# Low weight parts of every fourth chunk by a negated copy on ScalarE and an accumulating DMA, in a float32r two-part matmul kernel

## The reference

```
h    = rmsnorm(x) * norm_mix
proj = h @ w_in                      # 2048 x 4096: b, c, xt, v of 1024 each
y    = concat(b * conv3(c * xt), pool_scale * (pooled differences of v) @ pool_w)
x    = x + y @ w_out                 # 2048 x 2048
h    = rmsnorm(x) * norm_mlp
x    = x + relu(h @ w_up)**2 @ w_down   # 2048 x 8192, 8192 x 2048
out  = rmsnorm(x) * norm_final
```

## Time and profile before

| | |
|---|---|
| median of 3 runs | 1000.58 us (1000.52 to 1001.06) |
| profiled execution: its time | 1000.99 us |
| profiled execution: its span, first to last instruction | 999.2 us |
| mean granted TensorE clock | 0.996 |
| PE busy | 986.5 us |
| DVE busy | 586.4 us |
| ACT busy | 419.6 us |
| HBM read | 190.97 MB |

### The profile page before, as it was taken

One profiled execution on the slowest core, in us unless ns is written; L12 is line 12 of the kernel. 1 busy time (PEld: TensorE's weight loads), 2 busy tenths in 40 slices (PEclk: granted clock), 3 DMA queues, 4 the chain that ended last, 5 costly groups with the idle time before them and its releaser, 6 DMA issues.

```text
span 999.2 us, 12457 instructions
## 1 busy us (share of the span) xinstructions
PE 986.5 (99%) x5088; PEld 847.2 (85%) x5088; DVE 586.4 (59%) x428; ACT 419.6 (42%) x325; POOL 1.4 (0%) x9
## 2 busy tenths in 40 slices
PE   8999999999999999999999999999999999999996
PEld 7888888888888888888888888888888888888885
DVE  6597777655554766544656654556565445656453
ACT  6644435354443434333444433343433334444342
POOL 0000000000000000000000000000000000000000
PEclk9999999999999999999999999999999999999998
DMA  9956543555544655555455455545545554555512
GB/s 327 392 194 229 190 188 122 215 211 190 189 169 169 233 189 195 183 208 177 165 211 206 176 203 191 187 151 213 209 183 207 176 204 132 211 209 205 187 66 84
DMA packets 29694, 193.52 MB, mean 194 GB/s; under 512 B 3296, under 2 KB 3552, under 8 KB 7136
## 3 DMA queue, kind: packets, MB, share of 16 engines
q1 hardware_dynamic: 29232, 190.85, 52.1%
q10 hardware_dynamic: 288, 1.18, 0.3%
q0 software_dynamic: 144, 1.05, 0.3%
HBM read 190.97 MB, written 2.10 MB: 193 GB/s over the span
## 4 chain that ended last, share of the span: by engine, by line
PE 94%; DMA 3%; SPq 1%; DVE 1%; ACT 0%; issue 0%; ACTq 0%
PE ps L343 44%; PE ps L252 33%; PE ps L255 17%; DMA w_raw<-w_stream 3%; SPq L208 1%; PE ps L277 0%; PE ps L329 0%; SPq L193 0%; DVE w_lo L628 0%; ACT w_hi L449 0%; PE ps L317 0%; DVE val L635 0%; PE ps L276 0%; PE ps L279 0%; ACT cross L483 0%
## 5 line engine op out<-in xcount | busy, mean ns | idle before, releaser
L628 DVE TENSOR_TENSOR w_lo<-w_raw,w_hi 128x2048 fp32r<-128x2048 f32 x172 | 392.0, 2291 | 280.4 <-ACT w_hi L449 279.7
L449 ACT ACTIVATE w_hi<-w_raw 128x2048 fp32r<-128x2048 f32 x172 | 326.8, 1912 | 344.0 <-PE ps L343 210.8
L252 PE MATMUL ps<-act_a,w_hi 128*128 128x512 f32 x1472 | 351.1, 391 | 0.0
L343 PE MATMUL ps<-w_hi,act_b 128*128 128x512 f32 x1280 | 345.3, 390 | 0.0
L252 PEld LDWEIGHTS ps<-act_a,w_hi 128*128 128x128 f32 x1472 | 271.0, 188 | 52.5
L343 PEld LDWEIGHTS ps<-w_hi,act_b 128*128 128x128 f32 x1280 | 239.8, 188 | 49.3
L343 PE MATMUL ps<-w_lo,act_b 128*128 128x512 f32 x640 | 199.7, 389 | 0.0
L255 PEld LDWEIGHTS ps<-act_a,w_lo 128*128 128x128 f32 x1472 | 188.6, 191 | 7.0
L255 PE MATMUL ps<-act_a,w_lo 128*128 128x256 f32 x1472 | 191.1, 283 | 0.0
L343 PEld LDWEIGHTS ps<-w_lo,act_b 128*128 128x128 f32 x640 | 120.2, 188 | 25.0
L635 DVE TENSOR_TENSOR val<-ps,cross 128x1024 f32<-128x1024 f32 x26 | 31.8, 1223 | 47.2 <-ACT cross L455 47.2
(11 more groups left out here) (68 smaller groups left out, 164.3 us busy)
## 6 DMA issues: line engine op xcount, KB each, us to landing
w_raw<-w_stream SPq DMA_DIRECT2D x172, 1024.0 KB, 4.8
w_raw<-w_stream SPq DMA_DIRECT2D x16, 256.0 KB, 7.9
x<-x_rows SPq DMA_DIRECT2D x2, 1024.0 KB, 17.4
mix_mem<-x_t SPq DMA_DIRECT2D x3, 512.0 KB, 8.2
out<-x SPq DMA_DIRECT2D x6, 256.0 KB, 2.7
mix_mem<-pool_w ACTq DMA_DIRECT2D x1, 1024.0 KB, 9.1
mix_mem<-g_final POOLq DMA_DIRECT2D x1, 1024.0 KB, 5.0
out<-val SPq DMA_DIRECT2D x2, 256.0 KB, 2.1
```

The source lines that it names most:

```text
L252: return pe.matmul(ps[:, bank, :], weights_hi, act, start=first, stop=False)
L343: mm = pe.matmul(ps[:, NT * parity + t, :], a[:, at:at + P], cols, start=first and i == 0, stop=last and i == 2)
L449: act.activation(w_hi[:, c, :], w_raw[:, c, :], ACT.Copy).then_inc(hi_ready, 1)
L628: dve.tensor_tensor(out=w_lo[:, c, :], in0=w_raw[:, c, :], in1=w_hi[:, c, :].bitcast(F32), op=ALU.subtract)\
```

## The change

For chunk 3 of every block but the first, ACT, right behind its high part, also writes `w_lo` = float32r(-w_raw) with a copy scaled by -1, and increments a new semaphore `neg_ready`. GpSimd waits for it (`lo_of_last`) and issues a DMA that adds the raw weights of that chunk, read from HBM once more, to `w_lo` in SBUF; its landing increments `lo_last` by 16. DVE's subtraction for these chunks goes, and `lo_ready` now counts three chunks in a block. In block 0 the last piece's subtraction stays on DVE and increments `lo_first`. All waits for the low part, on PE and before SyncE's loads, go through a function `wait_lo` that picks the semaphore. GpSimd's 43 issues are written out one by one: that of block 1 stands before its memset of u's pads, those of blocks 2 to 12 before its load of `g_final`, the rest behind.

```diff
+        def wait_lo(engine, n, c):
+
+            if c == CHUNKS - 1 and isinstance(n, int) and n == 0:
+                engine.wait_ge(lo_first, 1)
+            elif c == CHUNKS - 1:
+                engine.wait_ge(lo_last, 16 * n)
+            else:
+                engine.wait_ge(lo_ready, (CHUNKS - 1) * n + (c + 1))
...
             def load_chunk(n, c):
-                sp.wait_ge(lo_ready, 4 * n + (c - 3))
+                wait_lo(sp, n - 1, c)
...
+            def lo_of_last(n):
+
+                pool.wait_ge(neg_ready, n)
+                pool.dma_start(w_lo[:, 3, :], w_stream[4 * n + 3, :, :],
+                               accum_op=ALU.add).then_inc(lo_last, 16)
+
             pool.wait_ge(x_lo_ready, KT)
             pool.memset(v[:, :, 0:PAD], 0.0).then_inc(v_pads_zero, 1)
+            lo_of_last(1)
             pool.wait_ge(pool_w_ready, 1)
             pool.memset(u[:, :, 0:2], 0.0).then_inc(u_pads_zero, 1)
-
+            for n in range(2, FIRST_OUT + 1):
+                lo_of_last(n)
             pool.wait_ge(value_ready, 2)
             pool.dma_start(g_row, g_final[0:1, :].to_broadcast([P, D])).then_inc(g_loaded, 16)
+            for n in range(FIRST_OUT + 1, BLOCKS):
+                lo_of_last(n)
...
-                    pe.wait_ge(lo_ready, 4 * n + (c + 1))
+                    wait_lo(pe, n, c)
...
                 act.activation(w_hi[:, c, :], w_raw[:, c, :], ACT.Copy).then_inc(hi_ready, 1)
+                if c == CHUNKS - 1:
+                    act.activation(w_lo[:, c, :], w_raw[:, c, :], ACT.Copy, scale=-1.0).then_inc(neg_ready, 1)
...
             def split(n, c):
 
+                if c == CHUNKS - 1:
+                    return
                 dve.wait_ge(hi_ready, 4 * n + (c + 1))
...
+                if k == KT - 1:
+                    op.then_inc(lo_first, 1)
+                else:
+                    op.then_inc(lo_ready if is_last(k) else piece_lo, 1)
```

More of the change, by code:

```diff
@@ L113, in build @@
         lo_ready = sem("lo_ready")
+        neg_ready = sem("neg_ready")
+        lo_first = sem("lo_first")
+        lo_last = sem("lo_last")
         chunk_used = sem("chunk_used")
@@ L379, in _ @@
                 if is_last(k):
-                    pe.wait_ge(lo_ready, k // CK + 1)
+                    wait_lo(pe, 0, k // CK)
                 else:
@@ L433, in _ @@
                         pe.wait_ge(act_ready, 4 * PARTS + 4 + (c + 1))
-                        pe.wait_ge(lo_ready, 4 * (BLOCKS - 1) + (c + 1))
+                        wait_lo(pe, BLOCKS - 1, c)
                     for k in range(CK):
@@ L722, in _ @@
                     dve.wait_ge(piece_hi, k - k // CK + 1)
-                dve.tensor_tensor(out=w_lo[:, k // CK, piece(k)], in0=w_raw[:, k // CK, piece(k)],
-                                  in1=w_hi[:, k // CK, piece(k)].bitcast(F32), op=ALU.subtract)\
-                   .then_inc(lo_ready if is_last(k) else piece_lo, 1)
+                op = dve.tensor_tensor(out=w_lo[:, k // CK, piece(k)], in0=w_raw[:, k // CK, piece(k)],
+                                       in1=w_hi[:, k // CK, piece(k)].bitcast(F32), op=ALU.subtract)
+                if k == KT - 1:
+                    op.then_inc(lo_first, 1)
+                else:
+                    op.then_inc(lo_ready if is_last(k) else piece_lo, 1)
             for c in range(CHUNKS):
```

## The result

The changed kernel takes 1018.38 us, the median of 4 runs (1017.77 to 1018.82), beside 1000.55 us for the kernel before. The ratio is 1.0172, 95% interval 1.0158 to 1.0187. The forecast was slower, 1012.6 us, range 1002 to 1035. The profiled execution took 1018.07 us; its span is 1016.2, 17.0 more than before.

The account below looks back on a forecast made before the run. PE's products were taken as the bound, busy 986.5 of 999.2 us. Stalls of 7.5 + 3.8 + 0.7 = 12.0 us on the profiled 1000.99 gave 1013.0, as a median 1012.6 us; range 1002 to 1035.

Parts of the forecast that it names:

- L: Time from the end of ACT's negated copy to the accumulate's landing: 8.0 us taken, range 5.3 to 10.7.
- (b): Row block behind feature block, chunk 3: room 6.5 us, PE stalls 1.5 us, five times, 7.5 us in all.
- (d): Last block, chunk 3, walked one token half at a time: room 4.2 us, PE stalls 3.8 us, everything behind shifts.
- R2: Rival: the accumulate takes three times a plain load's packet time; 1030 us, chance 0.20.
- (e): First norm: the negated copy delays ACT's square root, so PE waits 0.7 us more.
- (a): Feature block behind feature block, 14 such blocks: room 10.7 us for the low part, so no stall.
- (c): Row block behind row block, chunk 3: room 12.3 us for the low part, so no stall.
- the queues: SyncE's loads wait for the accumulate and g_final's load stands behind 12 accumulates; nothing late, no cost.
- R1: Rival: the accumulate costs as a plain load, landing about 5.3 us after the negated copy; 1002.4 us, chance 0.14.
- R3: Rival: the transfer becomes the bound at four times the packets, landing after 13.4 us; 1102 us, chance 0.10.
- R5: Rival: nothing happens, the low part is hidden everywhere; needs landing below 4.2 us in the last block; chance 0.02.
- R4: Rival: less DVE traffic in SBUF speeds PE's products, some 11.5 us back; about 991 us, chance 0.02.

Follow-up runs that it names:

- norm ahead: The kernel before, without accumulates, with the first norm's root and steps moved ahead of ACT's split (1,3) and DVE's splits (1,2) and (1,3): 1001.40 us, ratio 1.0010.

## Why the prediction was right, and where it was short

**The whole.** The direction, the mechanism and the places were right: PE waits in the fourth chunk of five row blocks and in the last block, and nowhere else beyond the first norm. It was 12.0 us by the steps and is 17.0 in the span, 17.8 between the medians.

**Removed DVE work at no gain.** Right; shown with 34 accumulates left, where the row blocks' products cost what they did and the ratio is 1.0009.

**L = 8.0 us.** Nearly right. Its parts were 0.3 to the issue and 7.7 to landing; measured 0.3 and 8.0, so L is 8.3. The doubling of the packets' time is shown by the plain loads: 3.1 against 5.7 us. The Trainium skill's "DMA: Bandwidth & Descriptors", "Rules for kernel authors", has the accumulate read its destination and write it later. The doubled time fits a second read, which the packets don't show; no run separates the read from the addition itself. My plain load was 5.0, and 5.1 was measured.

**(b), the five row blocks.** 7.5 us predicted, 9.6 measured. The room of 6.5 us was right; 0.3 of L and 0.1 us of slower first products at each place make the difference.

**(d), the last block.** This is the step that failed: 3.8 us predicted as a shift of everything behind it. The wait was 4.2, and I had the products behind it run at their old pace. They ran at half the clock for 6 us and cost 2.9 us more. The prediction had no term for what a wait does to PE's clock, at either place. It didn't matter at waits of 1.3 to 1.8 us in row blocks, where the first four products alone cost 0.1 us more, and did at 4.2. Had the accumulate been slower, the forecast for R2 (29.4 us) would likely have missed by more: with waits of 3.5 to 3.8 us in the row blocks the slow products cost 10 us over those of the changed kernel. That the waits here stayed short of this is luck as far as the prediction goes.

**(e), the first norm.** 0.7 predicted, 0.3 measured. Counted from the start of the high part (1,3), the root is 5.03 us later in place of 4.35, 0.7 as said; the loads before it landed 0.4 us earlier in this execution.

**(a), (c) and the queues.** Right: no wait there, and no new one for w_raw (ACT's waits for it in the splits, all at the start, are 2.7 us beside 4.1). The DMA share over the four row blocks is 0.78, about the 0.8 forecast. The loads land in 6.4 us where I had kept 4.8, which nobody waited for. That the held-back load leaves the engines to the accumulate was said in passing; it is worth about a microsecond at each of the five row blocks.

**Rivals.** R1 (L of 5.3) is what the plain loads do, 1002.6 us against 1002.4 worked out, with the 1.1 us of the last block as said. R2, R3 and R5 fall with L. R4 falls with the run that has 34 fewer subtractions and the same products.

**Still open.** What decides whether the clock falls behind a wait, and how long it stays down. The rows below give no one limit.

## What to carry to other kernels

Offloading an engine pays only where somebody waits for that engine; where its share is large but its results come early, the new path's latency is all that counts. Work it out per block against the moment of need, with the accumulate at twice a plain DMA's engine time (5.7 against 3.1 us here), and look first at the places where the order of work restarts: here a change of block kind and the last block. A late operand costs more than its wait, since PE may come back at half its clock.

## What the runs showed that was not expected

After a wait PE's clock may stay at 0.50 for 3 to 6 us. In row blocks and the last block waits of 0.85 to 2.2 us left it at 1.00 (five of 1.3 to 1.8 in the changed kernel, one of 2.16 and one of 2.17 in the last block), and those of 3.5 us and more (five of 3.5 to 3.8, then 4.05, 4.6 and 5.96) were all followed by slow products. What these cost doesn't follow the length of the wait: in the last block it was 2.9 us behind 4.05, 2.1 behind 4.6 and 1.6 behind 5.96.

At the first norm, after a start in which PE also waits at other places, no length of wait divides the two cases. In the profiled executions the clock stayed at 1.00 behind waits of 1.37 (the changed kernel), 1.54 (before), 1.89 (all six places on DVE) and 2.56 us (negated copy first), and fell to 0.50 behind 1.86 (plain loads), 1.97, 2.16, 2.31, 2.33, 2.56 (norm ahead) and 4.33 us (negated copy twice). The wait of 2.56 us after which it stayed up, beside the 3.27 us that the same 16 low products took behind 2.31:

```profile
48.50 0.71 PE L343 MATMUL ps<-inv_rms,ones 128*128 128x128 f32 x4 [2.56 <-DVE val L665]
48.97 2.15 PE L281 MATMUL ps<-act_a,w_lo 128*128 128x256 f32 x16
```

A fall there cost 1.5 us each time: from the end of the wait to the start of the 53rd product behind it are 9.5 us with it and 8.0 without. It may be why executions of one kernel differ by a microsecond or two: with the norm ahead, the four with a mean granted clock of 0.995 took 1001.75 to 1003.67 us and the seven with 0.997 to 0.999 took 1000.95 to 1001.42. Only one of the eleven has a trace, so this is not shown.
